# Turned blocks exchanged through device memory, in place of TensorE transposes for ten quarters

## The reference, cut to what matters

```
first block:   merged = sigmoid(gate_a) * ya + sigmoid(gate_b) * yb
               h = x + merged @ w_out              # 2048 x 2048; h is the residual
               z = rmsnorm(h, norm_ffn_g)
               h = h + (silu(z @ w_ffn_gate) * (z @ w_ffn_up)) @ w_ffn_down   # width 5632
second block:  o_mla = (mla_y * silu(mla_z)) @ w_mla_out      # the gated latent output, 256 x 2048
               merged = sigmoid(g_conv) * o_conv + sigmoid(g_mla) * o_mla + sigmoid(g_mem) * o_mem
               x = x + merged @ w_o                # merged: the second merged sum, 256 x 2048
```

## Time and profile before

| | |
|---|---|
| median of 3 runs | 2521.51 us (2520.6 to 2521.63) |
| the profiled execution | 2521.5 us, of it 2519.7 us span |
| busy: PE, PE weight load, DVE, ACT | 2504.8, 2064.6, 1539.8, 1134.8 us |
| granted TensorE clock | 1.0 in all 40 slices (the level of 2.4 GHz) |
| transfers | 472.22 MB, mean 187 GB/s |

### The profile page before, as it was taken

One profiled execution on the slowest core, in us unless ns is written; L12 is line 12 of the kernel. 1 busy time (PEld: TensorE's weight loads), 2 busy tenths in 40 slices (PEclk: granted clock), 3 DMA queues, 4 the chain that ended last, 5 costly groups with the idle time before them and its releaser, 6 DMA issues. The chain is left out here.

```text
span 2519.7 us, 29675 instructions
## 1 busy us (share of the span) xinstructions
PE 2504.8 (99%) x11502; PEld 2064.6 (82%) x11502; DVE 1539.8 (61%) x2101; ACT 1134.8 (45%) x1441; POOL 0.2 (0%) x4
## 2 busy tenths in 40 slices
PE   9999999999999999999999999999999999999999
PEld 7877778888888888878888888888888888888887
DVE  5666664465656555557656764557557767665554
ACT  5444434444444444433545444434435555544443
POOL 0000000000000000000000000000000000000000
PEclk9999999999999999999999999999999999999999
DMA  9655456665676767656556556565665555556554
GB/s 270 204 174 156 134 165 195 195 211 188 179 219 211 233 201 212 198 166 228 195 192 205 188 178 175 166 184 187 190 187 179 156 171 172 159 179 184 186 190 135
DMA packets 254268, 472.22 MB, mean 187 GB/s; under 512 B 23146, under 2 KB 45840, under 8 KB 253744
## 3 DMA queue, kind: packets, MB, share of 16 engines
q1 hardware_dynamic: 252912, 466.25, 59.5%
q10 hardware_dynamic: 1216, 4.07, 0.5%
HBM read 459.90 MB, written 2.49 MB: 184 GB/s over the span
## 5 line engine op out<-in xcount | busy, mean ns | idle before, releaser
L1563 DVE TENSOR_TENSOR w_lo<-raw,w_hi 128x1024 fp32r<-128x1024 f32 x864 | 1040.6, 1219 | 794.4 <-ACT w_hi L1144 778.2
L1144 ACT ACTIVATE w_hi<-raw 128x1024 fp32r<-128x1024 f32 x864 | 905.1, 1055 | 1119.3 <-PE acc L523 995.7
L521 PE MATMUL acc<-w_hi,x_hi_A 128*128 128x512 f32 x1880 | 743.9, 396 | 3.4 <-DVE w_lo L1563 3.4
L523 PE MATMUL acc<-w_hi,x_lo_A 128*128 128x512 f32 x1880 | 732.8, 390 | 0.0
L522 PE MATMUL acc<-w_lo,x_hi_A 128*128 128x512 f32 x1880 | 732.0, 389 | 0.0
L521 PE MATMUL acc<-w_hi,x_hi_B 128*128 128x512 f32 (+1 forms) x1216 | 472.2, 388 | 0.1
L523 PE MATMUL acc<-w_hi,x_lo_B 128*128 128x512 f32 (+1 forms) x1216 | 470.0, 387 | 0.0
L522 PE MATMUL acc<-w_lo,x_hi_B 128*128 128x512 f32 (+1 forms) x1216 | 469.8, 386 | 0.0
L521 PEld LDWEIGHTS acc<-w_hi,x_hi_A 128*128 128x128 f32 x1880 | 353.0, 188 | 87.6 <-issue 11.3
L523 PEld LDWEIGHTS acc<-w_hi,x_lo_A 128*128 128x128 f32 x1880 | 352.9, 188 | 74.8
L522 PEld LDWEIGHTS acc<-w_lo,x_hi_A 128*128 128x128 f32 x1880 | 353.3, 188 | 70.8 <-issue 0.5
(11 more groups left out here) (270 smaller groups left out, 1244.3 us busy)
## 6 DMA issues: line engine op xcount, KB each, us to landing
raw<-in_w_in_dram SPq DMA_DIRECT2D x376, 512.0 KB, 4.0
raw<-in_w_ffn_gate_dram SPq DMA_DIRECT2D x88, 512.0 KB, 4.5
raw<-in_w_ffn_up_dram SPq DMA_DIRECT2D x88, 512.0 KB, 4.4
raw<-in_w_ffn_down_dram SPq DMA_DIRECT2D x88, 512.0 KB, 4.0
raw<-in_w_out_dram SPq DMA_DIRECT2D x32, 512.0 KB, 4.6
raw<-in_w_mem_kv_dram SPq DMA_DIRECT2D x32, 512.0 KB, 5.2
raw<-in_w_mla_out_dram SPq DMA_DIRECT2D x32, 512.0 KB, 4.6
raw<-in_w_o_dram SPq DMA_DIRECT2D x32, 512.0 KB, 4.7
```

What stands on the lines that cost most here:

```text
L521: mm(o, xh, hi[:, k, :], start=(kt == first_k), stop=False)
L523: last = mm(o, xl, hi[:, k, :], start=False, stop=(kt == (last_k or c.kts) - 1))
L1144: ins = act.activation(w_hi[:, s, 0:n], raw[:, r, 0:n], ACT.Copy)
L1563: ins = dve.tensor_tensor(w_lo[:, s, 0:n], raw[:, r, 0:n], w_hi32[:, s, 0:n], ALU.subtract)
```

## The change

Ten quarters (the residual's first three, all four of `silz`, the second merged sum's first three) are no longer turned on PE. For each, DVE transposes 32 x 32 blocks with two instructions (`turn_blocks`), SP writes the 512 KB to device memory in one transfer (`put_...`), waits until it has landed, and reads it back in four transfers of 128 KB with the blocks exchanged (`get_...`). ACT waits for all four and makes the high part from SBUF, DVE the low part (`high_turned`, `low_turned`, or with a gain for the residual), and only then go both on with the next chunk's first granule. The fourth quarter of the residual and of the sum stays on PE. The hidden layer's and the memory's moves go through device memory too, in five transfers in place of 16, and the last hidden one moves from the first to the second `mem_k` chunk. In the diff "..." marks what is left out.

```diff
@@ SP
-            def move_hidden(i, b):
-                if b == 0:
-                    sp.wait_ge(hid_turned, i + 1)
-                for q in range(4):
-                    sp.dma_start(ff_rows[32 * b:32 * b + 32, i, :, q, :],
-                                 squares[32 * q:32 * q + 32, i % 2, :, b, :]).then_inc(hid_moved[i % 2], 16)
...
+            def put_blocks(region, src, written):
+                sp.dma_start(bass.AP(scratch.tensor, region * P * BLOCK, [[BLOCK, P], [1, BLOCK]]),
+                             src).then_inc(written, 16)
+            def get_blocks(region, dst, bs, moved):
+                for b in bs:
+                    rows = bass.AP(scratch.tensor, region * P * BLOCK + b * (BLOCK // 4), [[BLOCK, 32], [32 * BLOCK, 4], [1, BLOCK // 4]])
+                    sp.dma_start(dst[32 * b:32 * b + 32], rows).then_inc(moved, 16)
...
+            def put_xres(k):
+                sp.wait_ge(xres_turned, k + 1)
+                put_blocks(k % 2, xres_squares[k].rearrange("p t b n -> p (t b n)"), xres_written)
+            def get_xres(k, bs):
+                if bs[0] == 0:
+                    sp.wait_ge(xres_written, 16 * (k + 1))
+                for b in bs:
+                    rows = bass.AP(scratch.tensor, (k % 2) * P * BLOCK + b * P, [[BLOCK, 32], [CW, T], [32 * BLOCK, 4], [1, P]])
+                    sp.dma_start(xres_rows[k][32 * b:32 * b + 32], rows).then_inc(xres_moved, 16)
...
@@ SP, after the transfer of each granule g of a chunk
-                            if g < 4 and c.name == "ffn_gate" and 2 <= i < 6:
-                                move_mem(i - 2, g)
-                            if g >= 4 and c.name == "ffn_up" and i > 0:
-                                move_hidden(i - 1, g - 4)
-                            if g >= 4 and last_hidden is not None:
-                                move_hidden(last_hidden, g - 4)
+                            at = c.col // CW
+                            if (c.name == "w_out" and at >= 2) or (c.name == "ffn_gate" and i == 0):
+                                k = at - 2 if c.name == "w_out" else 2
+                                if g == 5:
+                                    put_xres(k)
+                                elif g > 5:
+                                    get_xres(k, (2 * g - 12, 2 * g - 11))
+                            if (c.name == "mla_out" and at >= 2) or (c.name == "w_o" and at == 0):
+                                k = at - 2 if c.name == "mla_out" else 2
+                                if g == 5:
+                                    put_total(k)
+                                elif g > 5:
+                                    get_total(k, (2 * g - 12, 2 * g - 11))
+                            if c.name == "gm":
+                                gm = (c.col - C2["gm"]) // CW
+                                if (gm, g) == (1, 5):
+                                    put_silz(0)
+                                    put_silz(1)
+                                elif (gm, g) == (1, 6):
+                                    get_silz(0)
+                                elif (gm, g) == (1, 7):
+                                    get_silz(1)
+                                elif (gm, g) == (2, 6):
+                                    put_silz(2)
+                                    put_silz(3)
+                                elif (gm, g) == (2, 7):
+                                    get_silz(2)
+                                elif (gm, g) == (3, 0):
+                                    get_silz(3)
...
+                            if (c.name == "ffn_up" and i > 0) or (c.name == "mem_k" and c.col):
+                                done = i - 1 if c.name == "ffn_up" else FF // CW - 1
+                                if g == 5:
+                                    put_hidden(done)
+                                elif g > 5:
+                                    get_hidden(done, (2 * g - 12, 2 * g - 11))
@@ PE
             for k in range(3):
-                with_turn(next_one("w_out"), cols(xres, k))
+                one("w_out")
             with_turn(chunks[0], cols(xres, 3), (0, 2, 4, 6))
...
-            background("gm", "gm", "gm")
-            back(GM_FIRST)
-            for j in range(KT // 4):
-                turn_quarter(cols(silz, j))
-                for k in GM_BACK[j]:
-                    back(k)
-            one("gm")
+            for _ in range(4):
+                one("gm")
             activations()
-            product_and_turn("mla_out", merged2, "w_o")
+            for _ in range(4):
+                one("mla_out")
+            with_turn(next_one("w_o"), cols(merged2, 3), (0, 2, 4, 6))
@@ ACT, the residual (the sum alike, with high_turned)
-            product_and_turn("B", GCOL["norm_ffn_g"])
+            for k in range(4):
+                if k:
+                    W.some(3)
+                    act.wait_ge(act_req, W.R.at(1))
+                    act.wait_ge(xres_moved, 64 * k)
+                    for j in range(4 * k - 4, 4 * k):
+                        ins = act.activation(XH["B"][:, j, :].rearrange("p (a c) -> p a c", c=32), xres_turn[k - 1][:, j % 4], ACT.Copy,
+                                             scale=gcol[:, GCOL["norm_ffn_g"] + j:GCOL["norm_ffn_g"] + j + 1])
+                    ins.then_inc(act_done, 1)
+                    W.R.next()
+                plain()
+                W.some(1)
...
@@ DVE
+            def turn_blocks(squares_, src):
+                for t in range(T):
+                    ins = dve.transpose(squares_[:, :, t].rearrange("p b (k c) -> p b k c", c=32),
+                                        src[:, t, :].rearrange("p (k b c) -> p b k c", k=4, c=32))
+                return ins
+            def low_turned(dst, turned, kt):
+                for t in range(T):
+                    lo, hi = (x[dst][:, kt:kt + 4, t * P:(t + 1) * P].rearrange("p k (q c) -> p k q c", q=4) for x in (XL, XH))
+                    ins = TT(lo, turned[:, t], hi.bitcast(F32), ALU.subtract)
...
             for k in range(4):
+                if k:
+                    W.some(3)
+                    ask_high()
+                    dve.wait_ge(act_done, W.R.next())
+                    for j in range(4 * k - 4, 4 * k):
...
+                        ins = STT(lo, xres_turn[k - 1][:, j % 4], gcol[:, g:g + 1], hi.bitcast(F32), ALU.mult, ALU.subtract)
...
+                    activations()
                 take_add(cols(xres, k))
-                turned_quarter("B", k, GCOL["norm_ffn_g"], meanwhile=lambda: row_part(xres, k))
+                if k < 3:
+                    turn_blocks(xres_squares[k].rearrange("p t b n -> p b t n"), cols(xres, k)).then_inc(xres_turned, 1)
+                    dve.wait_ge(xres_turned, k + 1)
+                    W.some(1)
+                    row_part(xres, k)
+                else:
+                    turned_quarter("B", 3, GCOL["norm_ffn_g"], meanwhile=lambda: row_part(xres, 3))
...
@@ DVE, the gm chunks
+            for k in range(4):
+                if k < 2:
+                    for j in (2 * k, 2 * k + 1):
+                        turn_blocks(silz_squares[j % 2], cols(silz, j)).then_inc(silz_turned, 1)
+                        dve.wait_ge(silz_turned, j + 1)
+                take_sigmoid()
+                if k < 2:
+                    for j in (2 * k, 2 * k + 1):
+                        ask_high()
+                        dve.wait_ge(act_done, W.R.next())
+                        low_turned("B", silz_turn[:, j], 4 * j)
```

More of the change, by code:

```diff
@@ L327, in build @@
         mem_turn = area(48, 4).rearrange("p (a k c) -> p k a c", k=4, c=32)
-        squares = stage[:].rearrange("p (z t) (b n) -> p z t b n", z=2, b=4)
+        xres_squares = [area(8 * k, 4).rearrange("p (t b n) -> p t b n", t=T, b=4) for k in range(3)]
+        xres_rows = [area(8 * k + 4, 4).rearrange("p (t q n) -> p t q n", t=T, q=4) for k in range(3)]
+        xres_turn = [area(8 * k + 4, 4).rearrange("p (a k c) -> p k a c", k=4, c=32) for k in range(3)]
+        squares = stage[:].rearrange("p (z h) (b t n) -> p z (h b) t n", z=2, b=2, t=T)
         fin_g = area(8, 8)
@@ new lines, in body @@
+                            if c.name == "ffn_gate" and 2 <= i < 6:
+                                if g == 0:
+                                    put_mem(i - 2)
+                                elif g < 3:
+                                    get_mem(i - 2, (2 * g - 2, 2 * g - 1))
+                            if (c.name == "ffn_up" and i > 0) or (c.name == "mem_k" and c.col):
[4 more added lines that the diff above has]
+                                    get_hidden(done, (2 * g - 12, 2 * g - 11))
@@ L1167, in norm_split, with product_and_turn @@
                     split_unit(dst, kt0 + 2 * p, gain + 2 * p)
-            def product_and_turn(dst, gain=None):
+            def product_and_turn(dst):
                 for k in range(4):
@@ L1173, in product_and_turn, with high_turned @@
                     for p in range(2):
```

(53 more changed lines are left out.)

104 lines of the change are left out of this document (74 added, 30 removed).

## The result

The changed kernel takes 2549.61 us, median of four runs (2545.76 to 2550.29); the kernel before took 2521.19 in four runs beside it. The ratio is 1.0109, interval 1.0098 to 1.0121: **28.4 us slower**. The forecast, 2527.0 with a range of 2512.5 to 2539, was wrong by 22.6 us, and the range did not hold the time. The profiled execution took 2549.29 us, of it 2547.5 us span.

The account below looks back on a forecast made before the run. The prediction took PE's instruction stream, end to end, as the bound. It summed 2521.5 - 8.9 (transposes) - 2.7 (hidden move) + 9.5 (residual) + 6.35 (sum) + 1.2 (`gm`) = 2527.0 us, range 2512.5 to 2539.

Parts of the forecast that it names:

- the six named places: PE gaps of 1 to 6 us starting `w_out` and `mla_out` chunks 2 and 3, first `ffn_gate` and `w_o` chunks.
- The gains: Ten quarters of transposes leaving PE save 8.9 us; the last hidden move, one `mem_k` chunk later, saves 2.7.
- The rival by which a transpose is worth 272 ns: Removed PE transposes gain their shown duration, 21.8 us in place of 8.9, giving 2514; chance 0.05.
- the cover of an exchange: Residual and sum exchanges land after PE's four-granule lead: 9.5 us lost in the residual, 6.35 in the sum.
- The write and the read: In each exchange through device memory, the write takes 4.3 us (2.7 to 5.5), the read 3.3 (3.1 to 4.4).
- The 1.3 us by which the second and third gap should be longer: PE starts those chunks with one split granule, not four, so the write leaves 1.3 us later.
- `gm`: In the `gm` chunks transfers are covered, but DVE's low part of g6 comes late: 1.2 us lost, bounds 0 and 2.5.
- Moves of the hidden layer and the memory: Five SP issues in place of 16, covered by at least three granules (8 us): priced at nothing.
- the third: Rival: exchange lateness at the high end or over, as weights, writes and reads delay each other; 2540, chance 0.07.
- Rival 1: Residual and sum exchanges land in their cover, leaving only the gains and `gm`: 2511, chance 0.18.

Follow-up runs that it names:

- the last hidden move alone: The kernel before, with only the 16 transfers of the last hidden chunk moved to the second `mem_k` chunk: 2518.22 us, ratio 0.9988.
- the best version: "take after the add" plus DVE handing the fourth quarter to PE before taking the third, and one low part ahead of the norm: 2509.45 us, ratio 0.9954.
- the `gm` version: The changed kernel with the six exchanges of residual and second merged sum undone, their quarters turned on PE again: 2514.76 us, ratio 0.9973.
- Filling the gaps: The changed kernel with 16 (residual) or 18 (sum) idle PE matmuls ahead of each of the six chunks: 2543.29 us, ratio 1.0092.
- take after the add: The changed kernel with ACT and DVE taking an exchanged quarter of residual and sum after the next chunk's add, same transfers: 2511.9 us, ratio 0.9963.
- the earlier-issue kernel: The changed kernel with each residual or sum write behind g4, not g5, and all four reads behind g5, not g6 and g7: 2518.12 us, ratio 0.9988.

## Why the prediction was wrong

The direction and the mechanism of the gaps were right: six gaps behind DVE's low parts at the six named places, with ACT's waits for transfers ahead of each. The gains were right too: 8.9 and 2.7 where the starts give 9.1 and 3.0, borne out by the last hidden move alone (3.3) and by the best version (11.3 for both). The rival by which a transpose is worth 272 ns would have given the `gm` version 8.7 us from its 32 transposes and 11.4 in all; it gained 6.9.

**The step that failed is "the cover of an exchange"**, by two terms: the gaps came to 27.9 us and not 15.85, and what follows a gap was not priced at all.

1. *The write and the read were too cheap: the six gaps are 12.1 us longer, 2.1 in the residual and 10.0 in the sum.* I took 4.3 and 3.3 us. The residual's writes took 5.0 to 5.1, its last reads 3.9 to 4.7; the sum's took 6.4 to 7.3 and 5.0 to 5.8. For the residual's first quarter, in time into the chunk (from 556.5): the write left at 9.2 (predicted 9.35), the last read landed at 20.9 (predicted 19.15), PE had its granule 5.0 later (predicted 4.9), and PE was through the chunk at 21.8 as I had it. The 1.9 us by which this gap is longer are the write (0.7), the read (0.7) and the last read's issue, half a microsecond late. In the sum's first quarter the write took 3.0 us more than I took and the last read 1.7, and the gap is 4.9 longer; the last landings came 23.5, 24.6 and 24.5 us into the chunks. My bounds for the write ended at 5.5, the median of three writes of results, while the same row has 7.3 as its slowest: the bound was drawn from the middle of a row where it should have gone to its end. With 7.3 and 4.4 the sum's gaps would have come to 5.3, 6.6 and 6.6 (18.5 in all), nearer to the 16.3 measured than my 6.35 was. The read has a reason that the changed kernel's own rows show: two reads of each quarter stand right behind the weight g7, and took 3.9 to 5.8 us, where of the twelve ahead of it eleven took 2.5 to 3.2.
2. *The clock behind a gap was not in the sum at all, 12.0 us in slow steps.* I wrote that PE's time is its stream plus its waits, and left the pace behind a wait at 0.227 without a reason. The kernel before shows 1.0 in every slice, and it has no such gap. Filling the gaps won back only 6 to 7 us of this; in the account, where the gaps are counted as measured, all 12 stand beside them.

The 1.3 us by which the second and third gap should be longer did not show (4.18, 4.18, 3.26). The write did leave later in those chunks, at 11.1 and 10.3 us in place of 9.2, but the slow steps at their head kept PE 2.5 and 1.6 us longer in them, which is more. Where the fills kept the clock up the second and third were longer, by 0.6 and 0.8.

**`gm`** cost 0 and not 1.2. The low part of granule 6 was done at 2296.9 and PE wanted it at 2297.4, which leaves 0.5 us; I had it 1.2 late. Moves of the hidden layer and the memory cost nothing, as said.

**The rival nearest to the result** was the third, the lateness at or over its high end, with a chance of 0.07. Its reason, that the transfers delay each other, is half right: a write that takes 2.7 us alone takes 4.9 to 7.7 between weights, over all these kernels. The section "Latency and other measured facts" of the page "DMA: Bandwidth & Descriptors" in the Trainium skill has the fixed cost of a transfer grow with the load on device memory; these rows fit it, though they can't tell that cost from the queueing behind a weight. That this alone makes the loss is refuted by "take after the add". Rival 1, the covered exchange at 2511, had the wrong time for this kernel, but it is what the kernel does when its wait stands elsewhere: 2511.9.

**What the forecast should have asked** was what one microsecond more would do. A lateness of 2.3 us was the difference between a cover of 21.8 and a chain of 24.05, of which the exchange was 10 and not well known; it counts six times, and each gap brings the clock with it. The upper side of the range had to be far wider than the lower one.

## What to carry to other kernels

Put the consumer of an exchange through device memory behind the next piece of independent work, not at the point where the pipeline's lead is just as long as the exchange; here the same transfers cost 37.7 us more or less by that alone. Cost a write and a read in series by the slowest rows of transfers between weights (here 11.5 to 14.6 us from the write's issue to the last landing), not by medians, and multiply the miss by the number of exchanges. Issue all reads of an exchange together, ahead of the next weight. Where PE gets gaps of several microseconds, add what the matmuls behind them cost at the lower clock (here 2 us a gap); a profile without such gaps can't show that cost.

## What the runs showed of the hardware that I had not expected

- Behind each of the six gaps (3.3 to 6.1 us in which PE did nothing) PE ran about ten steps of 0.43 us at a granted clock near 0.5, some 2 us a gap; around the wait of 0.78 us in the earlier-issue kernel (at 601.92) the clock stayed at 1.00 (view by windows, PE alone: us, busy, clock, transfer share, GB/s):

```profile
600.00:604.00 4.00, 3.22 (x15) 1.00 0.21 47
604.00:608.00 4.00, 4.00 (x19) 1.00 1.03 369
```

- One transfer of 512 KB into device memory took 5.0 us at one place and 7.3 at another, without regard to its region. In all six it landed 1.1 to 1.4 us after the weight issued just ahead of it. Why that weight took 4.3 us at one place and 6.5 at the other is not settled.
- A read of 128 KB right behind a weight took 3.9 to 5.8 us in the changed kernel; with the next weight issued behind all four reads, 2.5 to 3.0 in 23 of 24 (the other 3.6).
- Sixteen direct moves are no quicker than the hop by way of device memory when one queue issues them: 0.63 us each, 3.1 us a granule with its weight, against 2.72 that PE takes.
